# Feed-forward layers of a two-block transformer: most gate and up columns computed transposed, with weight blocks stationary and the activations moving

## The reference, cut to what matters

```python
def swiglu(h, wg, wu, wd):
    return (jax.nn.silu(h @ wg) * (h @ wu)) @ wd
# D_MODEL = 1024, D_FF = 2816, SEQ = 256
h = rms_norm(x, ffn1_norm[l])                       # first stack
x = x + 0.5 * swiglu(h, wg[l], wu[l], wd[l])
n = _modulate(_rms_norm(h, norm_g[l, 0]), sh1, sc1) # second stack
h = h + 0.5 * ga1 * _swiglu(n, ffn_w_in[l, 0], ffn_w_out[l, 0])
```

## Time and profile before

| what | value |
|---|---|
| runs of the kernel before | 2198.57 us median of 3 (2198.44 to 2198.6) |
| profiled execution | 2198.41 us, span 2196.6 us |
| PE | 2174.4 us busy, 99% of the span |
| DVE | 1514.4 us busy, 69% |
| ACT | 1117.2 us busy, 51% |
| granted TensorE clock | 1.000 of full speed (2.4 GHz) over the span |

### The profile page before, as it was taken

How to read it: one execution, slowest core, us unless ns; L and a number is a source line. 1 busy time by engine, 2 the same in 40 slices (tenths; PEclk the granted TensorE clock), 3 DMA queues, 4 the chain that set the end, 5 groups by cost and what they waited for, 6 DMA issues and landing times.

```text
span 2196.6 us, 26628 instructions
## 1 busy us (share of the span) xinstructions
PE 2174.4 (99%) x10692; PEld 1816.6 (83%) x10692; DVE 1514.4 (69%) x2307; ACT 1117.2 (51%) x1733; POOL 25.9 (1%) x32
## 2 busy tenths in 40 slices
PE   8999999999999999999999999999999999999998
PEld 7888888888888888888888887888888888778887
DVE  5655974556875977877876555888688765558564
ACT  5445654344445654445445656544454456656443
POOL 0000010000000010000000000000000000000000
PEclk9999999999999999999999999999999999999999
DMA  8554455556884557876886444588768864445653
GB/s 294 193 203 149 148 181 174 192 197 216 285 300 157 157 184 268 282 258 208 280 279 214 139 152 134 199 271 278 268 225 286 284 197 153 144 140 182 230 201 125
DMA packets 252785, 462.91 MB, mean 211 GB/s; under 512 B 11943, under 2 KB 57937, under 8 KB 252533
## 3 DMA queue, kind: packets, MB, share of 16 engines
q1 hardware_dynamic: 252420, 461.05, 62.3%
q10 hardware_dynamic: 240, 0.16, 0.0%
HBM read 460.12 MB, written 1.05 MB: 210 GB/s over the span
## 4 chain that ended last, share of the span: by engine, by line
PE 91%; DVE 6%; ACT 2%; issue 0%; DMA 0%; POOL 0%; ACTq 0%; POOLq 0%; DVEq 0%
PE ps L1858 19%; PE ps L1861 18%; PE ps L1859 18%; PE s L1858 8%; PE s L1861 8%; PE s L1859 8%; PE ps L1831 4%; DVE wl L2470 2%; DVE cacc L2681 1%; PE s L1987 1%; PE ps L1874 1%; PE ps L1872 1%; PE ps L1873 1%; PE ps L2013 1%; DVE gts L2854 1%; ACT pt L2268 1%
## 5 line engine op out<-in xcount | busy, mean ns | idle before, releaser
L2470 DVE TENSOR_TENSOR wl<-raw,wh 128x1024 fp32r<-128x1024 f32 (+2 forms) x740 | 856.1, 1185 | 134.4 <-ACT wh L2178 130.9
L2178 ACT ACTIVATE wh<-raw 128x1024 fp32r<-128x1024 f32 (+2 forms) x740 | 732.2, 1031 | 395.5 <-PE ps L1861 134.8
L1858 PE MATMUL ps<-wh,xh 128*128 128x512 f32 (+3 forms) x1600 | 613.9, 384 | 1.5 <-DVE wl L2470 1.5
L1861 PE MATMUL ps<-wh,xl 128*128 128x512 f32 (+3 forms) x1600 | 603.1, 377 | 0.0
L1859 PE MATMUL ps<-wl,xh 128*128 128x512 f32 (+3 forms) x1600 | 602.9, 377 | 0.0
L1858 PEld LDWEIGHTS ps<-wh,xh 128*128 128x128 f32 x1600 | 300.5, 188 | 58.2 <-issue 10.1
L1861 PEld LDWEIGHTS ps<-wh,xl 128*128 128x128 f32 x1600 | 300.4, 188 | 48.5
L1859 PEld LDWEIGHTS ps<-wl,xh 128*128 128x128 f32 x1600 | 300.7, 188 | 45.7
L2478 DVE SCALAR_TENSOR_TENSOR acc<-raw,condT,acc 128x512 f32<-128x512 f32 x252 | 188.8, 749 | 5.1
L2261 ACT ACTIVATE hTh<-ps 128x512 fp32r<-128x512 f32 x88 | 48.3, 596 | 217.0 <-PE ps L1831 217.0
L2605 DVE TENSOR_TENSOR hTl<-ps,hTh 128x512 fp32r<-128x512 f32 x88 | 57.1, 687 | 140.2 <-ACT hTh L2261 140.1
(11 more groups left out here) (355 smaller groups left out, 2415.5 us busy)
## 6 DMA issues: line engine op xcount, KB each, us to landing
raw<-in_ffn_w_in SPq DMA_DIRECT2D x80, 1024.0 KB, 5.4
raw<-in_ada_w SPq DMA_DIRECT2D x72, 1024.0 KB, 6.2
raw<-in_ffn_wg SPq DMA_DIRECT2D x40, 1024.0 KB, 5.3
raw<-in_ffn_wu SPq DMA_DIRECT2D x40, 1024.0 KB, 5.5
raw<-in_ffn_wd SPq DMA_DIRECT2D x40, 1024.0 KB, 5.8
raw<-in_ffn_w_out SPq DMA_DIRECT2D x40, 1024.0 KB, 6.7
raw<-in_mix_w_in SPq DMA_DIRECT2D x28, 1024.0 KB, 5.2
raw<-in_w_in SPq DMA_DIRECT2D x28, 768.0 KB, 4.5
```

Of the source, the lines that this page charges most:

```text
L1858: e.matmul(o, X[0](kk, t), hi, start=kk == 0, stop=False)
L1861: ins = e.matmul(o, X[1](kk, t), hi, start=False, stop=kk == K - 1)
L2178: ins = self.e.activation(m.wh[j % NH][:, 0:n], m.raw[u % NR][:, k0 * w:k0 * w + n], ACT.Copy)
L2470: ins = self.e.tensor_tensor(m.wl[j % NH][:, 0:n], m.raw[u % NR][:, k0 * w:k0 * w + n], hi, ALU.subtract)
```

## The change

In each feed-forward the first 512 columns stay as they are. The other 2304 columns of gate and up are done in nine steps p of 256 columns each. A unit is now 8 row blocks by 256 columns, a sub 4 row blocks by 256. For each row block and each 128 columns the `wh` block is stationary and xh and xl (now side by side in one tile `xx`) move together in 512 columns, then the `wl` block is stationary and xh moves in 256. A PSUM bank then holds in its first half wh.xh + wl.xh and in its second half wh.xl, with the hidden columns on the partitions. ACT copies the second halves out, DVE adds the first halves, ACT takes the silu, and the product is split into `hTh` by an ACT copy and `hTl` by a DVE subtraction, with no transposes of `hb` for these columns. In the first stack the row factor of the gate is a tile `rB` made by two matmuls, and that of up is moved to the final addition to x.

```diff
@@ Weights.ffn
-        for c in range(5):
-            self.gemm(label + "g", Wg, 8, (g0 + 512 * c, 512))
-            self.gemm(label + "u", Wu, 8, (f0 + 512 * c, 512))
-        for k0 in (0, 4):
-            self.units.append(dict(kind="w", label=label + "gu", nk=4, w=512, per=2, src=[
-                (wview(Wg, k0, 4, g0 + 2560, 256), 0, 256), (wview(Wu, k0, 4, f0 + 2560, 256), 256, 256)]))
+        self.gemm(label + "g", Wg, 8, (g0, 512))
+        self.gemm(label + "u", Wu, 8, (f0, 512))
+        for p in range(9):
+            for n, W, c0 in (("G", Wg, g0), ("U", Wu, f0)):
+                self.units.append(dict(kind="w", label=label + n, nk=8, w=256, per=4, src=[
+                    (wview(W, 0, 8, c0 + 512 + 256 * p, 256), 0, 256)]))
@@ Order.ffn
+        def columns(label, b, after=lambda: None):
+            for k in (0, 4):
+                j, hs, _, _ = self.take(label)
+                self.turned_sub(j, hs, k, b)
+                self.ahead()
+                for _ in range(2):
+                    self.setup_more()
+                if k == 0:
+                    self.flush(1)
+                    after()
+            return self.s.sub, j
...
+        for p in range(9):
+            bg, bu = banks(), banks()
...
+            tg = columns(label + "G", bg, self.lo_of_last)
+            if p == 0:
+                if rs:
+                    self.spread_rr()
+                self.turn_h(0)
...
+            self.gate_turned(p, bg, tg, rs, glow, gsum, gate)
+            self.free[bg[0]] = self.free[bg[1]] = gsum
...
+            tu = columns(label + "U", bu, set_up)
...
+            self.up_turned(p, bu, tu, gate, ulow, usum, up, hi)
+            self.free[bu[0]] = self.free[bu[1]] = usum
+            self.hb_free[4 + p % 2] = hi
+            self.last_hi = p, hi
@@ Tensor
+    def turned_sub(self, j, hs, k0, b):
+        m, s, e = self.m, self.s, self.e
+        self.wait_ge(self.lo_at[j])
+        for k in range(4):
+            kk = k0 + k
+            both, x_hi = m.xx[:, kk, :, :].rearrange("p a s -> p (a s)"), m.xx[:, kk, 0, :]
+            for n in range(2):
+                c = slice(k * 256 + n * P, k * 256 + (n + 1) * P)
+                o = m.ps[b[n]]
+                self.wait_ge(self.x_hi.get(kk), self.x_lo[kk], self.free[b[n]] if kk == 0 else None)
+                if kk < 7:
+                    e.matmul(o, m.wh[hs][:, c], both, start=kk == 0, stop=False)
+                    ins = e.matmul(o[:, 0:S], m.wl[hs][:, c], x_hi, start=False, stop=False)
...
+    def spread_part(self, b, diag, tk, done):
+        m = self.m
+        self.wait_ge(diag, self.free[b])
+        for t in range(2):
+            ins = self.e.matmul(m.ps[b][:, t * P:(t + 1) * P], m.ones, m.rd[:, t, :], start=True, stop=True)
+        self.then_inc(ins, tk)
@@ Scalar
+    def gate_turned(self, p, b, tg, rs, glow, gsum, gate):
+        m = self.m
+        g = m.sg[p % 2][:, :]
+        self.wait_ge(tg, self.sg_free[p % 2])
+        self.then_inc(self.e.activation(g.rearrange("p (n s) -> p n s", n=2), m.halves(b)[1], ACT.Copy), glow)
+        self.wait_ge(gsum)
+        self.then_inc(self.e.activation(g, g, ACT.Silu), gate)
+
+    def up_turned(self, p, b, tu, gate, ulow, usum, up, hi):
...
+        self.then_inc(self.e.activation(u, m.halves(b)[1], ACT.Copy), ulow)
+        self.wait_ge(up)
+        self.then_inc(self.e.activation(m.hTh[:, 4 + 2 * p:6 + 2 * p, :].rearrange("p k s -> p (k s)"), m.hb[1][p % 2][:, :],
+                                        ACT.Copy), hi)
@@ Vector
-            ins = e.scalar_tensor_tensor(out=xs, in0=m.ps[b], scalar=0.5, in1=xs, op0=ALU.mult, op1=ALU.add)
+            ins = e.scalar_tensor_tensor(out=xs, in0=m.ps[b], scalar=m.rh[:, t:t + 1], in1=xs, op0=ALU.mult, op1=ALU.add)
...
+    def spread_part(self, b, diag, tk, done):
...
+        for t in range(2):
+            ins = self.e.tensor_scalar(m.rd[:, t, :], m.ident, m.rr[:, t:t + 1], None, ALU.mult)
...
+    def gate_turned(self, p, b, tg, rs, glow, gsum, gate):
...
+        self.wait_ge(glow)
+        ins = e.tensor_tensor(g, m.halves(b)[0], g, ALU.add)
         if rs:
...
+            self.wait_ge(self.own(ins, "gate sum"), self.r_spread)
+            ins = e.tensor_tensor(g, g, m.rB[:, :].unsqueeze(1).broadcast_to([P, 2, S]), ALU.mult)
+        self.then_inc(ins, gsum)
+
+    def up_turned(self, p, b, tu, gate, ulow, usum, up, hi):
...
+        self.wait_ge(ulow)
+        self.then_inc(e.tensor_tensor(u, m.halves(b)[0], u, ALU.add), usum)
+        self.wait_ge(usum, gate)
+        self.then_inc(e.tensor_tensor(u, u, g, ALU.mult), up)
+
+    def low_turned(self, p, hi, done):
...
+        self.wait_ge(hi)
+        self.then_inc(self.e.tensor_tensor(lo, m.hb[1][p % 2][:, :], h.bitcast(F32), ALU.subtract), done)
```

More of the change, by code:

```diff
@@ L258, in __init__ @@
         self.rr = sb("rr", [P, 4])
+        self.rh = sb("rh", [P, 2])
         self.top += (self.x_at - self.top) % 512
@@ L276, in __init__ @@
         self.acl = sb("acl", [P, 512], F32R)
+        self.rB = sb("rB", [P, S])
         self.top = u0
@@ L341, in __init__, with halves @@
         self.ps = [self.two[b // 2][:, 512 * (b % 2):512 * (b % 2) + 512] for b in range(8)]
+    def halves(self, b):
+        both = self.two[b[0] // 2][:, :].rearrange("p (n h s) -> p n h s", n=2, h=2)
+        return both[:, :, 0, :], both[:, :, 1, :]
     def at(self, name, shape, dt, at):
@@ L434, in __init__ @@
         self.rows_scaled = None
+        self.last_hi, self.r_spread = None, None
         self.depth = FFN_DEPTH
@@ L997, in banks, with rows @@
             return b
-        def whole(label, b):
+        def rows(label, b):
             k = 0
@@ L1006, in whole @@
                     self.flush(1)
-            return td
-        rs = s is None
[L1010 to L1048, removed]
@@ new lines, in rows @@
+                yield k, td
+        def columns(label, b, after=lambda: None):
[9 more added lines that the diff above has]
+            return self.s.sub, j
+        rs = s is None
+        bg, bu = banks(), banks()
+        if rs:
+            for _, tg in rows(label + "g", bg):
+                pass
+        else:
+            tg = self.skewed(label + "g", bg)
@@ new lines, in ffn, with set_up @@
+        for _, tu in rows(label + "u", bu):
+            pass
+        for t in range(2):
+            done = self.new(self.s.vec, "up")
+            gated = self.new(self.s.act, "gate")
+            self.gate(t, bg[t], 512, tg, rs, gated)
+            self.up(0, t, bg[t], bu[t], 512, tu, gated, done)
+            self.sg_free[t] = self.free[bg[t]] = self.free[bu[t]] = done
+            self.up_at[0] = done
+        for p in range(9):
+            bg, bu = banks(), banks()
+            glow, gsum, gate = self.new(self.s.act, "glow"), self.new(self.s.vec, "gsum"), self.new(self.s.act, "tgate")
+            ulow, usum, up, hi = (self.new(a, n) for a, n in ((self.s.act, "ulow"), (self.s.vec, "usum"),
+                                                               (self.s.vec, "tup"), (self.s.act, "thi")))
+            tg = columns(label + "G", bg, self.lo_of_last)
+            if p == 0:
+                if rs:
+                    self.spread_rr()
+                self.turn_h(0)
+            if p == 1 and nx[0] == "final":
+                self.load_gain(nx[1])
+            self.gate_turned(p, bg, tg, rs, glow, gsum, gate)
+            self.free[bg[0]] = self.free[bg[1]] = gsum
+            def set_up():
+                if not self.set_up and p in (1, 2):
+                    self.setup_rest(2 * p - 2)
+            tu = columns(label + "U", bu, set_up)
+            if not self.set_up and p == 1:
+                self.setup_rest(1)
+            elif not self.set_up and p == 2:
+                self.angles()
+                self.set_up = True
+            self.up_turned(p, bu, tu, gate, ulow, usum, up, hi)
+            self.free[bu[0]] = self.free[bu[1]] = usum
+            self.hb_free[4 + p % 2] = hi
+            self.last_hi = p, hi
@@ L1959, in first_rest, with turned_sub @@
             self.then_inc(ins, (s.sub, j))
+    def turned_sub(self, j, hs, k0, b):
+        m, s, e = self.m, self.s, self.e
[10 more added lines that the diff above has]
+                    ins = e.matmul(o[:, 0:S], m.wl[hs][:, c], x_hi, start=False, stop=False)
+                else:
+                    e.matmul(o[:, 0:S], m.wl[hs][:, c], x_hi, start=False, stop=False)
+                    ins = e.matmul(o, m.wh[hs][:, c], both, start=False, stop=True)
+        self.then_inc(ins, (s.sub, j))
+    def spread_part(self, b, diag, tk, done):
[4 more added lines that the diff above has]
+        self.then_inc(ins, tk)
     def h_part(self, c, i, b, tk, th, tl):
@@ L2586, in add_part, with up, spread_part, gate_turned @@
         self.then_inc(ins, done)
-    def up(self, c, t, bg, bu, w, tu, gated, rs, done):
+    def up(self, c, t, bg, bu, w, tu, gated, done):
         m = self.m
```

(33 more changed lines are left out.)

32 lines of the change are left out of this document (28 added, 4 removed).

## The result

The changed kernel takes 2239.99 us (median of 4 runs, 2238.31 to 2240.95) against 2198.59 for the kernel before in the same measurement: ratio 1.0185, 95% interval 1.0173 to 1.0197. It is 41.4 us slower; 45.3 had been forecast. The profiled execution took 2238.31 us.

What follows compares the result with a forecast made beforehand. PE bound the kernel before; afterwards a DVE and ACT loop of waits would bind in feed-forwards with ada units. 2198.4 + 15.3 - 31.3 + 1.8 + 59.5 = 2243.7, rounded to 2244 us; range 2182 to 2266.

Steps and rivals of the forecast that it cites:

- The mechanism and its place: Nine steps: twice a step DVE's next `wl` waits 1.68 us for ACT's silu or high copy, then `wh`.
- The loss by feed-forward: Five feed-forwards with ada units: 15.8 us in each first-stack one, 9.3 in each second-stack one, 59.5 in all.
- DVE's sum: DVE's nine steps in feed-forwards with ada units: 115.4 us in the second stack, 122.3 in the first.
- nothing more is lost: Down projection: DVE needs about 2.0 us a sub against PE's 2.72, so it catches up.
- TensorE's part: PE alone: 15.3 us more for added matmuls, 31.3 less for turns, 1.8 more for the spread, giving 2184.2 us.
- the pair: PE's turned steps: a 512-column matmul at 226.6 ns and a 256-column one at 119.8, together 346.4 ns.
- The stock: Splits made ahead of PE: PE feels only what of DVE's lag goes beyond them, taken as 3.3 us.
- Rival 1: DVE and ACT's loop does not bind in the steps, PE sets the time: 2184 us; chance 0.16.
- Rival 2: PE's 256-column matmuls cost up to 173 ns because their load is not hidden: 2308 us; chance 0.06.
- Rival 3: Landings become the wait, 0.5 us for each of 90 turned units, 45 us: 2289 us; chance 0.07.
- Rival 4: Stalls of about 14 us in all cancel the gain, within 0.2% of before: 2198 us; chance 0.03.
- The light feed-forwards: First two and last feed-forwards: DVE's loop 2.5 and 1.3 us above PE, loss counted as 0.

Runs made afterwards that it cites:

- Experiment 1: Changed kernel with both ScalarE copies (gate's silu and hidden columns' high copy) written behind the next high split: 2192.68 us, ratio 0.9967 to the kernel before.
- experiment 4: Changed kernel with splits four subs ahead of TensorE in the feed-forwards, not three: 2236.53 us, ratio 1.0168 to the kernel before.
- experiment 11: Experiment 1 with the two 512-column products of each row block first, then the two of 256: 2191.29 us, ratio 0.9961 to the kernel before.
- experiment 5: Changed kernel with splits four subs ahead, not three, and reductions taken up three subs late, not one: 2227.70 us, ratio 1.0125 to the kernel before.
- experiment 7: Changed kernel with turned units reading 4 row blocks of 512 columns in 2 KB rows, not 8 of 256 in 1 KB: 2240.05 us.

## Why the prediction was right

- **The mechanism and its place** were as forecast: the silu and the high copy, waiting for DVE, held back the next `wh`, and DVE stood idle twice a step. Idle of 1.64 us against 1.68; a step without ada units 10.55 us against 10.60 in the second stack, 11.27 against 11.29 in the first. Experiment 1 keeps all work, takes the waits away, and the 47.3 us go.
- **The loss by feed-forward.** The changed kernel and experiment 1 have the same instructions on PE in the same order, so the distance between the two profiles can be read at the first and the last matmul of each feed-forward's nine steps (us; experiment 1's profile started 2.0 us later, so the 46.9 us of the table are 44.9 between the two spans):

| feed-forward | forecast | lost in the nine steps | lost from there to the next one's steps |
|---|---|---|---|
| first and second (no ada units) | 0 | 1.0 | 0.2 |
| third | 15.8 | 10.1 | 3.5 |
| fourth | 15.8 | 9.8 | 2.4 |
| fifth | 9.3 | 4.4 | 1.1 |
| sixth | 9.3 | 4.1 | 3.1 |
| seventh | 9.3 | 4.2 | 3.0 |
| last | 0 | 0.0 | 0.0 |
| sum | 59.5 | 33.6 | 13.3 |

- **The mis-sized term is DVE's sum** for the feed-forwards with ada units: 12.8 and 13.6 us a step (115.4 and 122.3 over nine), where the eight intervals average 12.3 to 12.6 in the second stack and 13.1 and 13.3 in the first. Over nine steps of five feed-forwards that is 15.8 us too much, where the loss was forecast 12.6 us too high. The items were right: in the fifth feed-forward 8 x 10.60 for the loop, 8 x 1.44 for the pairs outside the gaps and 2.4 for the reductions give 98.7 us, measured 98.6. What was counted too high is how much of the rest falls in: 2.4 to 3.3 us of reductions and not 4.3, eight or nine pairs between the first gate sum and the last and not ten, and the `hTl` of chunk 0 lies before the first of them.
- **One step failed: "nothing more is lost" in the down projection.** 13.3 us are lost behind the nine steps; PE's waits for `wl` go on there (9.1 us in 12 waits), and experiment 1 has none. Where a fourth sub is in stock and PE waits at the reductions in its place (experiment 4), only some 1 us is lost there and more in the steps. So the stock only puts off a part of the loss; it moves between the two places.
- **TensorE's part.** Fewer turns and more matmuls gave 2192.7 us where nothing stalls and not 2184.2. The mis-sized term is the pair, 350 ns and not 346.4: 8 x 9 x (11.20 - 11.09) = 7.9 us of the 8.5. This error and that of the loss nearly cancel, so that 2244 came closer than its terms were is luck. By the 2.5 ns of the Trainium skill (TensorE: Matmul & The Clock Gate, section Back-to-back issue gap) a pair would be an estimated 325 ns; the trace has 350, about 15 ns beyond the columns for each matmul. The same page's estimate of 107 ns for a load (section LDWEIGHTS) fits the pitch of 111 ns in the earlier trace rows; experiment 11 doesn't measure a load and shows only that it stays hidden behind 256 columns.
- **The stock.** That TensorE feels DVE's lag late by a stock of subs holds (experiment 5). A fourth sub alone was worth 3.5 us, since PE's order has the reductions in it and the clock fell at the end of four of their waits.
- **The rivals.** Rival 1 is what experiment 1 made true by another order, at 2192.7 and not 2184. Rival 2 falls with the pairs of 350 ns. Rival 3 falls with experiment 7. Rival 4, stalls of some 14 us, did not occur.
- **The light feed-forwards** were counted at zero, though the first stack's steps of 11.27 us are DVE's loop just above PE's 11.20. The first two lost 1.2 us together, all of it in the first.

## What to carry to other kernels

When two engines hand work back and forth in strict order, write out one period of both queues and add up what stands between a wait and the next item that a third engine needs; busy shares of 73% and 53% hid a loop that cost 47 us. An instruction that waits for the partner belongs behind the next piece of work that does not, here one high split later. And more stock helps only if nothing else in the bound engine's own order waits for the late engine; look at the granted clock too, for a wait of 3 us on TensorE was followed here by 3.4 us at half of it.

## What was not expected of the hardware

A pair of 512 and 256 columns took 347.0 ns in some stretches of one feed-forward and 354 in others, with the granted clock at 1.00 in both. The change comes with the units: with the copies moved (experiment 1) it is, from the third or fourth step on and but for a few mixed units, one rate for the gate's units and the other for those of `up` in each feed-forward, and which of the two is slow differs (`up` in the second to seventh feed-forward, the gate in the first and the last). The 350 ns of a step are thus a mean of two rates. The cause was not found, and the order of long and short did not matter.

The granted clock fell to 1.2 GHz at the end of four waits of 2.6 to 3.3 us of TensorE (experiment 4), for 3.4 us each time, and in no other profile before the end.

The first matmuls of 512 columns start some 12 us after the first instruction. In the changed kernel's profile they follow each other at 0.23 us from there on; in experiment 1's at 0.43 us until 16.2 us, and PE is then 2.0 us later. The executions of most kernels, the one before among them (2198.4 and 2200.4), lie 2 us apart too; whether that is this start was not looked at in more than one profile of each.

Transfers in rows of 1 KB came at 350 GB/s against 414 in two windows. Over more windows of 0.5 us with all DMA engines busy, 350 to 425 us in the profiles of the changed kernel and of experiment 7, the medians are 383 and 406 GB/s: a smaller difference, without any effect on the time.
